# A two-layer encoder trunk on one core: the first two token tiles in feature halves, the last one in column halves

## The reference

```
h = x
for l in 0, 1:
    mix = mixer_l(rmsnorm(h, mix_pre[l]))          # layer 0: conv + RG-LRU scan, gelu gate; layer 1: windowed attention
    h = h + rmsnorm(mix, mix_post[l])
    f = swiglu(rmsnorm(h, ffn_pre[l]))             # silu(h @ w_g) * (h @ w_u) @ w_down, inner width 2816
    h = h + rmsnorm(f, ffn_post[l])
rmsnorm(x, g) = x * rsqrt(mean(x * x) + 1e-6) * g
```

## Time and profile before

| | us |
|---|---|
| median of 3 runs | 1196.55 |
| lowest, highest | 1194.62, 1199.19 |
| the profiled execution | 1194.91 |
| its span, first to last instruction | 1193.1 |
| TensorE busy in it | 1150.5 (96%) |
| VectorE, ScalarE, GpSimd busy | 552.5, 451.7, 90.1 |

### The profile page before, as it was taken

How to read it: one execution, slowest core, us unless ns; L and a number is a source line. 1 busy time by engine, 2 the same in 40 slices (tenths; PEclk the granted TensorE clock), 3 DMA queues, 4 the chain that set the end, 5 groups by cost and what they waited for, 6 DMA issues and landing times.

```text
span 1193.1 us, 13470 instructions
## 1 busy us (share of the span) xinstructions
PE 1150.5 (96%) x5605; PEld 959.9 (80%) x5605; DVE 552.5 (46%) x688; ACT 451.7 (38%) x715; POOL 90.1 (8%) x73
## 2 busy tenths in 40 slices
PE   7999998999999999999998998999999999999997
PEld 6888886879888888888887877788888888888885
DVE  4867976665333333322237577437433333332223
ACT  5365465454232323221125467434422232322112
POOL 1003213300000000000022432000000000000000
PEclk9999999999999999999999999799999999999999
DMA  6332233313433333333323321122433333333311
GB/s 189 90 97 63 71 99 124 89 38 115 127 92 102 93 100 95 98 96 88 102 75 71 89 54 38 34 71 71 124 106 88 106 88 106 90 105 90 90 52 71
DMA packets 150798, 106.98 MB, mean 90 GB/s; under 512 B 23905, under 2 KB 140753, under 8 KB 150738
## 3 DMA queue, kind: packets, MB, share of 16 engines
q1 hardware_dynamic: 150402, 106.06, 30.7%
q10 hardware_dynamic: 336, 0.07, 0.0%
HBM read 104.01 MB, written 2.10 MB: 89 GB/s over the span
## 4 chain that ended last, share of the span: by engine, by line
PE 79%; DVE 13%; ACT 5%; issue 1%; POOL 1%; ACTq 0%; PEldq 0%; POOLq 0%
PE ps L1084 15%; PE ps L1086 15%; PE ps L1085 15%; PE ps L1103 10%; PE ps L1104 10%; PE ps L1107 10%; DVE xc L866 2%; PE ps L1113 1%; DVE w_lo L754 1%; DVE t_i L852 1%; ACT w_hi L470 1%; ACT s_sb L681 1%; PE ps L1299 1%; DVE xc_lo L875 1%; DVE root L848 1%
## 5 line engine op out<-in xcount | busy, mean ns | idle before, releaser
L754 DVE TENSOR_TENSOR w_lo<-raw,w_hi 128x1024 fp32r<-128x1024 f32 x176 | 220.8, 1255 | 526.2 <-ACT w_hi L470 526.1
L1084 PE MATMUL ps<-x_hi,w_hi 128*128 128x512 f32 (+1 forms) x1096 | 405.8, 370 | 6.8 <-DVE x_lo L765 2.5
L1085 PE MATMUL ps<-x_lo,w_hi 128*128 128x512 f32 (+1 forms) x1096 | 403.3, 368 | 0.0
L1086 PE MATMUL ps<-x_hi,w_lo 128*128 128x512 f32 (+1 forms) x1096 | 403.1, 368 | 0.0
L470 ACT CAST w_hi<-raw 128x1024 fp32r<-128x1024 f32 x186 | 194.7, 1047 | 444.6 <-PE ps L1086 260.5
L1084 PEld LDWEIGHTS ps<-x_hi,w_hi 128*128 128x128 f32 x1096 | 209.0, 191 | 42.2 <-issue 5.2
L1086 PEld LDWEIGHTS ps<-x_hi,w_lo 128*128 128x128 f32 x1096 | 209.0, 191 | 33.7
L1085 PEld LDWEIGHTS ps<-x_lo,w_hi 128*128 128x128 f32 x1096 | 209.1, 191 | 33.2
L1103 PE MATMUL ps<-w_hi,hid 128*128 128x512 f32 x352 | 139.1, 395 | 0.0
L1104 PE MATMUL ps<-w_lo,hid 128*128 128x512 f32 x352 | 138.9, 394 | 0.0
L1107 PE MATMUL ps<-w_hi,hid 128*128 128x512 f32 x352 | 110.3, 395 | 0.0
(11 more groups left out here) (144 smaller groups left out, 1087.3 us busy)
## 6 DMA issues: line engine op xcount, KB each, us to landing
raw<-in_ffn_w_gu SPq DMA_DIRECT2D x88, 512.0 KB, 3.8
raw<-in_ffn_w_down SPq DMA_DIRECT2D x44, 512.0 KB, 3.6
raw<-in_a_w_in SPq DMA_DIRECT2D x24, 512.0 KB, 4.3
raw<-in_a_w_out SPq DMA_DIRECT2D x12, 512.0 KB, 3.7
raw<-in_b_w_q SPq DMA_DIRECT2D x16, 256.0 KB, 3.7
raw<-in_b_w_o SPq DMA_DIRECT2D x16, 256.0 KB, 3.8
h<-in_x SPq DMA_DIRECT2D x4, 512.0 KB, 5.9
result<-h SPq DMA_DIRECT2D x4, 512.0 KB, 2.6
```

The costliest lines, as they stand in the source:

```text
L754: v.tensor_tensor(w_lo[:, t % 4, :], raw[:, t % 4, :], w_hi[:, t % 4, :].bitcast(F32), ALU.subtract)\
L1084: nc.tensor.matmul(out_ps, hi_w, hi_x, start=first, stop=False)
L1085: nc.tensor.matmul(out_ps, hi_w, lo_x, start=False, stop=False)
L1086: return nc.tensor.matmul(out_ps, lo_w, hi_x, start=False, stop=final)
```

## The change

START_PARTS cuts token tiles 0 and 1 into two halves of four feature blocks of 128 each; tiles 2 and 3 stay whole. Norm, turning, high and low part go by these parts, with semaphores of their own (first_hn, first_turned, first_hi, first_lo). The first half of a weight tile's products waits for the third part's low half, the second half for the fourth's. The parameter loads move from ScalarE's queue to SyncE's, behind weight tile 3. ScalarE takes the root of eps before it squares anything. w_lo of weight tile 0 moves from VectorE to GpSimd. At the end, the last token tile's products go column half by column half, each half has its own square, multiply by gpost and store, and reciprocal and addition are one instruction for each half. The sum of the second half's squares goes into the root, with the first half's sum plus eps as its bias. Counts that other places wait for are lowered by four.

```diff
+START_PARTS = [(0, 0, 4), (0, 4, 8), (1, 0, 4), (1, 4, 8), (2, 0, 8), (3, 0, 8)]
...
 # SyncE
-            for t in range(1, T_OUT):
+            for t in range(1, 4):
+                load_in(t)
+            sp.dma_start(r_rows[0:48, :], a_conv_w[0]...).then_inc(params_landed, 16)
+            ...   # four loads of 12 rows, two of 8 rows, and sinks_in
+            for t in range(4, T_OUT):
...
-            for t in range(TC):
+            for t in range(TC - 1):
                 sp.wait_ge(h_ready, 3 * TC + t + 1)
                 sp.dma_start(out[0, t * P:(t + 1) * P, :], h[:, t, :]).then_inc(out_stored, 16)
-            sp.wait_ge(out_stored, 16 * TC)
+            for half in range(2):
+                sp.wait_ge(h_ready, 4 * TC + half)
+                cols = slice(half * S, half * S + S)
+                sp.dma_start(out[0, S - P:S, cols], h[:, TC - 1, cols]).then_inc(out_stored, 16)
+            sp.wait_ge(out_stored, 16 * (TC + 1))
...
 # GpSimd
-            nc.gpsimd.memset(eps[:, :], EPS)
+            nc.gpsimd.memset(eps[:, :], EPS).then_inc(eps_ready, 1)
...
+            pool.wait_ge(w_hi_ready, 1)
+            nc.gpsimd.tensor_tensor(w_lo[:, 0, :], raw[:, 0, :], w_hi[:, 0, :].bitcast(F32), ALU.subtract)\
+                .then_inc(w_lo_ready, 1)
...
 # ScalarE
-            act.dma_start(r_rows[0:48, :], a_conv_w[0]...).then_inc(params_landed, 16)
-            ...   # the other seven parameter loads
+            act.wait_ge(eps_ready, 1)
+            nc.scalar.activation(std[:, 32:33], eps[:, 0:1], ACT.Sqrt)
...
+            def first_high(i):
+                t, k0, k1 = START_PARTS[i]
+                act.wait_ge(first_turned, i + 1)
+                nc.scalar.copy(x_hi[:, k0:k1, t * P:(t + 1) * P], turned_in(t)[:, k0:k1, :]).then_inc(first_hi, 1)
             square_x(0)
             square_x(1)
             split_hi(0)
-            x_high(-1, 0)
-            x_high(-1, 1)
+            for i in range(4):
+                first_high(i)
             square_x(2)
             split_hi(1)
             square_x(3)
-            x_high(-1, 2)
+            first_high(4)
             split_hi(2)
-            x_high(-1, 3)
+            first_high(5)
...
-            for t in range(TC):
+            for t in range(TC - 1):
                 post(3, t)
+            for half in range(2):
+                act.wait_ge(last_acc, half + 1)
+                nc.scalar.activation(junk[:, 0:S], bank(2 * TC - 2 + half), ACT.Square, scale=D ** -0.5,
+                                     accum_out=last_ss[:, half:half + 1]).then_inc(last_sq, 1)
+                act.wait_ge(last_sq, half + 1)
+                if half == 0:
+                    nc.scalar.activation(last_ss[:, 2:3], last_ss[:, 0:1], ACT.Identity, bias=eps[:, 0:1])\
+                        .then_inc(last_sum, 1)
+            act.wait_ge(last_sum, 1)
+            n = post_at(3, TC - 1)
+            nc.scalar.activation(std[:, n:n + 1], last_ss[:, 1:2], ACT.Sqrt, bias=last_ss[:, 2:3]).then_inc(std_ready, 1)
...
 # VectorE
+            def normalise_x(i):
+                t, k0, k1 = START_PARTS[i]
+                n = pre_at(-1, t)
+                r = reciprocal(n) if k0 == 0 else rstd[:, n:n + 1]
...
+                v.scalar_tensor_tensor(out=work[:, t % 2, cols], in0=h[:, t, cols], scalar=r, in1=acc(3)[:, cols],
+                                       op0=ALU.mult, op1=ALU.mult).then_inc(first_hn, 1)
+            for i in range(4):
+                normalise_x(i)
+            for i in range(4):
+                first_low(i)
+            normalise_x(4)
             split_lo(1)
-            normalise_x(3)
-            x_low(-1, 2)
+            normalise_x(5)
+            first_low(4)
             split_lo(2)
-            x_low(-1, 3)
+            first_low(5)
...
-            for t in range(TC):
+            for t in range(TC - 1):
                 after_post(3, t)
+            for half in range(2):
+                dve.wait_ge(last_sq, half + 1)
+                cols = slice(half * S, half * S + S)
+                v.tensor_tensor(work[:, 1, cols], bank(2 * TC - 2 + half), gpost[:, cols], ALU.mult)\
+                    .then_inc(last_steps, 1)
+            r = reciprocal(post_at(3, TC - 1))
+            dve.wait_ge(last_steps, 2)
+            for half in range(2):
+                cols = slice(half * S, half * S + S)
+                v.scalar_tensor_tensor(out=h[:, TC - 1, cols], in0=work[:, 1, cols], scalar=r, in1=h[:, TC - 1, cols],
+                                       op0=ALU.mult, op1=ALU.add).then_inc(h_ready, 1)
...
 # TensorE
-                    drain(b, 3, range(k0, n_tiles), *args)
+                    for half in range(2):
+                        tok = slice(S - P, S)
+                        for k in range(k0, n_tiles):
+                            ins = rows(first_tile + k, TC - 1, hi(k)[:, tok], lo(k)[:, tok], False, k == n_tiles - 1,
+                                       (half,))
+                        ins.then_inc(last_acc, 1)
...
+            def first_turn(i):
+                t, k0, k1 = START_PARTS[i]
+                pe.wait_ge(first_hn, i + 1)
+                for k in range(k0, k1):
+                    ins = nc.tensor.transpose(turned_in(t)[:, k, :], work[:, t % 2, k * P:(k + 1) * P], ident[:, :])
+                ins.then_inc(first_turned, 1)
+            def first_half(i):
+                tile_ready(i)
+                for part in range(2):
+                    pe.wait_ge(first_lo, 3 + part)
+                    columns(i, i, range(4 * part, 4 * part + 4), slice(0, S // 2))
+            for i in range(4):
+                first_turn(i)
+            first_half(0)
+            first_turn(4)
+            first_half(1)
+            first_turn(5)
+            first_half(2)
             pe.wait_ge(params_landed, 16 * 8)
             nc.tensor.transpose(ps[:, 3, 0:R_ROWS], r_rows[0:R_ROWS, :], ident[0:R_ROWS, 0:R_ROWS]).then_inc(rows_ready, 1)
+            pe.wait_ge(first_lo, 6)
             for i in range(3):
-                token_half(-1, i, 0, 1)
+                columns(i, i, tok=slice(S // 2, S)).then_inc(tiles_done, 1)
```

More of the change, by code:

```diff
@@ L245, in trunk @@
         xlo_ready = sem("xlo_ready")
+        eps_ready = sem("eps_ready")
+        first_hn = sem("first_hn")
+        first_turned = sem("first_turned")
+        first_hi = sem("first_hi")
+        first_lo = sem("first_lo")
+        last_acc = sem("last_acc")
+        last_sq = sem("last_sq")
+        last_sum = sem("last_sum")
+        last_steps = sem("last_steps")
         conv_ready = sem("conv_ready")
@@ L351, in _ @@
             load_x(3)
-            for t in range(1, T_OUT):
+            for t in range(1, 4):
+                load_in(t)
+            sp.dma_start(r_rows[0:48, :], a_conv_w[0].rearrange("w (c p) -> (w c) p", p=P)).then_inc(params_landed, 16)
+            for row, v in ((R_CONV_B, a_conv_b[0]), (R_BRG, a_b_rg[0].rearrange("n c -> (n c)")),
+                           (R_BIG, a_b_ig[0].rearrange("n c -> (n c)")), (R_LAM, a_lam[0])):
+                sp.dma_start(r_rows[row:row + 12, :], v.rearrange("(c p) -> c p", p=P)).then_inc(params_landed, 16)
+            for row, v in ((R_KV, kv_norm), (R_Q, mix_pre[1])):
+                sp.dma_start(r_rows[row:row + 8, :], v.rearrange("(c p) -> c p", p=P)).then_inc(params_landed, 16)
+            sp.dma_start(sinks_in[:, :], b_sinks[0:1, :].broadcast_to([P, HEADS])).then_inc(params_landed, 16)
+            for t in range(4, T_OUT):
                 if is_gate_tile(t):
@@ L479, in x_high @@
             def x_high(b, t):
-                act.wait_ge(turned, TC * (b + 1) + t + 1)
+                act.wait_ge(turned, TC * b + t + 1)
                 nc.scalar.copy(x_hi[:, :, t * P:(t + 1) * P], turned_in(t)).then_inc(xhi_ready, 1)
[L484 to L490, removed]
+            act.wait_ge(eps_ready, 1)
+            nc.scalar.activation(std[:, 32:33], eps[:, 0:1], ACT.Sqrt)
             def square_x(t):
@@ L766, in x_low, with first_low @@
                     .then_inc(xlo_ready, 1)
-            def normalise_x(t):
-                r = reciprocal(pre_at(-1, t))
-                if t == 0:
+            def normalise_x(i):
+                t, k0, k1 = START_PARTS[i]
+                n = pre_at(-1, t)
+                r = reciprocal(n) if k0 == 0 else rstd[:, n:n + 1]
+                if i == 0:
                     dve.wait_ge(gain_spread, 1)
                 if t >= 2:
[L774 to L783, removed]
+                    dve.wait_ge(first_turned, 2 * t - 2)
+                cols = slice(k0 * P, k1 * P)
+                v.scalar_tensor_tensor(out=work[:, t % 2, cols], in0=h[:, t, cols], scalar=r, in1=acc(3)[:, cols],
+                                       op0=ALU.mult, op1=ALU.mult).then_inc(first_hn, 1)
+            def first_low(i):
+                t, k0, k1 = START_PARTS[i]
+                dve.wait_ge(first_hi, i + 1)
+                tok = slice(t * P, (t + 1) * P)
```

(16 more changed lines are left out.)

21 lines of the change are left out of this document (9 added, 12 removed).

## The result

The changed kernel took 1183.91 us in the median of six runs (1181.09 to 1185.14), against 1197.2 for the one before, a ratio of 0.9892 with a 95% interval from 0.9876 to 0.9908. The forecast was 1189.5 and a range from 1186.5 to 1194.0.

What follows compares the result with a forecast made beforehand. TensorE was 79% of the span, its start bound by a ScalarE and VectorE chain. Span 1193.1 - 4.95 (start) - 2.15 (tail) = 1186.0, or 1189.5 us on the scale of the medians; range 1186.5 to 1194.

Steps and rivals of the forecast that it cites:

- Is the shift kept?: Between start and tail: same instructions with shifted semaphore counts, so the start's whole 4.95 us carries to the end.
- The start's first product: First product on TensorE at 11.75 instead of 16.07, 4.3 us earlier, once the third x_lo half is ready.
- The second token halves: Products of the other token halves start at 23.1 instead of 28.07, 4.95 us earlier.
- rival 2: Start: weight tiles 1 and 2 land 3 us later, absorbing about 1.8 of the gain; 1191.3 us, chance 0.05.
- The clock: TensorE's first products: no fall to the low level, 1.4 of the start's gain; otherwise a loss of about 1.5 us.
- Rival 1: Start gives only 2.5 to 4 through a clock fall or GpSimd's w_lo; 1191 to 1192 us, chance 0.22.
- the trace disagrees: Start: against the rule that transposes are no clock activity, eight products behind sixteen transposes ran at pitch 0.12 at once.
- GpSimd's w_lo: Start: w_lo of weight tile 0 takes 2.39 from 9.1, ending 11.5, hidden by only 0.2 us.
- The moved DMAs: Parameter loads on SP issued 11.9 to about 15.5, landing 18 to 19, needed at 23.0; cost zero.
- rival 4: Parameters land late and hold TensorE before the second token halves; at 37 the kernel takes 1203 us, chance 0.04.
- The tail: Behind the last product: last store issued 1.43 earlier and 0.7 shorter, 2.15 us together, bounds 1.4 to 2.3.
- Rival 3: Tail: the root's table is loaded again, so the tail gives 0.8; 1190.8 us, chance 0.05.

Runs made afterwards that it cites:

- e1: Kernel before with 64 unused bytes a partition between std and rstd, moving every tile from rstd on; ratio 0.9934, 7.9 us faster.
- e2: Changed kernel with std back to 32 columns and its new scratch tiles at the top of memory, other tiles in their old places; ratio 0.9951.
- e5: Kernel before with 32 unused bytes ahead of rstd; one profiled execution, 1195.32 us.
- e6: Kernel before with 128 unused bytes ahead of rstd; one profiled execution, 1186.13 us.
- e7: Kernel before with 64 unused bytes ahead of w_hi and 64 behind w_lo; one profiled execution, 1200.71 us.
- e8: Kernel before with 64 unused bytes ahead of raw, so weight tiles and hid move together and x stays; one profiled execution, 1206.74 us.
- s1: Changed kernel with the eight parameter loads back on ScalarE's queue, behind its early square root; one time, 1182.47 us.
- s2: Changed kernel without the early square root of eps; one time, 1185.50 us.
- s3: Changed kernel with w_lo of weight tile 0 back on VectorE instead of GpSimd; one time, 1182.76 us.
- f3: Changed kernel with all other tiles where they lay before, same source as e2, timed again; median 1190.8 us, ratio 0.9943.
- f4: The changed kernel a second time, unaltered; median 1182.82 us, ratio 0.989 to the kernel before.
- e3: The start of the change alone, against the kernel before, with tiles in their old places and the tail as before; ratio 0.9953, 5.6 us faster.
- the best version: Changed kernel with 64 more unused bytes ahead of rstd, bringing y and hid level with the weight tiles; 1179.48 us, ratio 0.9872.
- f1: Kernel before with 64 unused bytes ahead of rstd, same kernel as e1, timed again; median 1188.62 us, ratio 0.9935.

## Why the prediction was wrong

- **"Is the shift kept?" failed.** It said that the rest of the kernel is the same instructions, and took the middle at nothing, where 5.15 was measured; by the prediction's own signs a shift of the middle by more than 1 us meant that it was wrong. The instructions are the same, their operands' addresses are not. In the profiled execution the down stages gave 1.81 and 1.85 (between the same products), and the stages with y and o about 0.9 and 0.7 by their pitch, 5.3 together. Falls of the clock came out differently too, by 0.6 to 1.6 us a stage, in both directions, and nearly cancel here, which is luck. The pitch is shown by e1, e2 and e5 to e8. It was there to be read in the whole diff: std grew by one column and last_ss stood in the middle of the allocation. No rival had it.
- **The start's first product**: 11.66 against 11.75, each step within 0.2. Right.
- **The second token halves**: 22.46 against 23.1. The step that fixed weight tile 1 at 13.8 failed too; I kept the landing of before and left out what the removed packets do to it, though rival 2 asked about that in the other direction. It lands at 12.3; s1 shows 1.2 of the 1.5. So w_lo of tile 1 ended at 15.65 instead of 16.1 and the turning of tile 2 had no fall in it.
- **The clock.** No fall was taken, and in the profile there is none. That was partly luck: each of the nine profiled executions with the old start has a run of slow products among the first 72, but so do s1, s2, s3 and f3 with the new one. Rival 1's price for it, 1.5, is about what f3 shows: its second token halves start at 23.95, against 22.46 in the changed kernel and 22.18 in e2. With the old start they start between 27.76 and 29.15, so the gain of 5.6 is that of one pair of profiles.
- **The rule on transposes** of the Trainium skill, "TensorE: Matmul & The Clock Gate", section "PE-mode transpose": ten of the eighteen profiled executions, f3, s1, s2 and s3 among them, run at the low level right behind the transposes (pitch 0.21), and eight, among them the changed kernel, f4, e2, e3 and the best version, at the high level (0.12). Both occur, and in one and the same kernel (e2 and f3; e1 and f1). So the rule does not hold in every execution here, and the prediction's sentence that the trace disagrees, from before alone, was too strong.
- **GpSimd's w_lo**: 2.37, ended 0.3 before the first product. Right, and with it on VectorE the first product is 0.93 later (s3).
- **The moved DMAs**: issued 10.30 to 14.64, where 11.9 to 15.5 was worked out, and no wait for them. Right, rival 4 did not occur. What the prediction calls full rings shows in the trace as issues that get longer once five or six transfers of 512 KB are under way: the first six took 0.36 to 0.58 each, the next two 2.48 and 5.18 before, 2.20 and 3.80 after. The trace does not look into the queue itself.
- **The tail**: 1.94 against 2.15, the term that was off is mostly the half store, 2.1 instead of 1.9. Rival 3 did not occur: the Identity loads no table. The Trainium skill, "ScalarE: Activation LUTs", section on table sets, says identity is in every set, and here the trace agrees.

## What to carry to other kernels

When a diff adds or widens a tile, list what moves behind it before calling the rest unchanged: on this kernel 64 bytes were worth more, by an estimated 5 us, than the whole tail with 1.9. Where TensorE holds one fp32r operand and streams another over it at full pace, try the offsets between the two tiles: level by 256 bytes was the fastest of the distances tried here in every stage, and one line of padding gave it. A one-column activation that loads the right table while the first transfer is under way can take two loads off the path, one of which would have stood behind the wait (s2). And before a step of a few microseconds is put down to an edit, profile one kernel twice: the clock alone moved the start by 1.8 and the attention stage by 4.8.

## What the runs showed of the hardware

- The pitch of 512-column fp32r products depends on the relative addresses of the held and the moving tile: 0.2267 at distance 0, 0.2289 at 64, 0.2333 at 96, 0.2324 at 128, 0.2333 at 192 bytes modulo 256. Five of 56 stages at 64 or 128 ran at 0.2333 instead, one of them in a second execution of a kernel that had shown 0.2289.
- 336 small packets on ScalarE's queue delayed a 512 KB load on SP's by 1.2 to 1.5 us (8.6 against 9.8 and 10.1; 8.5 to 8.7 in eight executions without them, 9.6 to 10.1 in nine with the old start).
- The granted clock in the rows reads 1.00 from 11 to 15 us in s1, while its products run at a pitch of 0.21 until 15.6, little over half the pace of the changed kernel's 0.12. e2 and f3, the same kernel, differ in the same way. Early in an execution the pace of the products has to be looked at, not that column.
- Kernels that differ in nothing but addresses in the attention stage spent 99.7 to 104.8 us between the same two products of it; e1 and f1, the same kernel, 101.05 and 104.80, and e2 and f3, also one kernel, 99.94 and 104.76.
